# The first projection of the last MLP as seven block products instead of eight

## Chip, core and metric

The kernel runs on one core of one Trainium2 chip. The metric is the device time of one execution in microseconds (us). TensorE (PE) multiplies, VectorE (DVE), ScalarE (ACT) and GpSimd (POOL) do the rest, and SyncE (SP) issues most DMA transfers.

## What is computed

512 tokens of width 1024 pass a retention layer, a latent attention layer, and a block that ends in an MLP. Everything is float32 at the interface. The part that the change touches, cut from the reference:

```
h = rmsnorm(x, norm_mlp_g[l])
x = x + jnp.square(jax.nn.relu(h @ w_up[l])) @ w_down[l]   # h 512x1024, w_up 1024x4096
return rmsnorm(x, final_g)
```

## The kernel before

Every float32 product is made of three faster ones. An operand is split into a rounded part (hi) and the remainder (lo), and PE adds hi·hi, hi·lo and lo·hi in PSUM: `split_dots`, three matmuls of a 128x128 stationary tile. ACT makes hi by a rounding copy (`split_hi`, `copy`), POOL or DVE makes lo = value − hi (`split_lo`, `lo_of`). Weights come in panels of 128x2048 values (1 MB) through two stage tiles: SP loads a panel, ACT writes `whi`, POOL writes `wlo`, PE uses both. There is no scheduler: each engine runs the instructions in the order in which its part of the program is written, and semaphores hold it back.

The stages, in order of time: four heads of the retention layer (panels 0 to 23, six for each head), its output product AO, the latent attention with its output product BO, the local attention, the output product of the block (panels `WO` to `WO+3`), its norm, then the MLP: the first projection (panels `UP` to `UP+15`) and the second projection, DN.

AO, BO and DN are already made as seven block products in place of eight (Strassen's scheme in Winograd's form). Sums of weight blocks are made during earlier stages in DRAM: ACT copies blocks to `tsum` (`copy_blocks`), POOL adds others to them with accumulating DMA transfers (`sum_step`), of which each waits on a count of landed copies, `t_copy`. DVE makes the sums of the activation blocks.

The first projection is plain. 32 output tiles of 128 features are each the sum of 8 tiles along k, times 512 tokens: 24 matmuls 512 columns wide. The first three tiles are made in two halves of 256 tokens, because the tokens arrive a quarter at a time: DVE adds the last product to the residual (`gather(q)`), ACT sums the squares and takes the root (`root_mean_square(q)`), DVE scales (`scale(q)`, written to `h2_tok`), PE turns the quarter (`turn_x`, 8 transposes of 128x128), ACT rounds it to `xhi` and DVE writes `xlo` (`transposed(q)`). PE turns quarters 0 and 1 while it still multiplies for `WO`, begins the projection on them, and turns quarters 2 and 3 after 48 matmuls of it. For each tile ACT applies the relu from PSUM (`hidden`) and DVE squares it into `hid` (`squared`). Stage 3, `whi_a`, `wlo_a` hold a third set of weights where needed.

Of the kernel before, what the change touches and what calls it, by code (L numbers as in the profile page):

```python
# [64 lines left out]
APART = (B0, L0, UP)  # L65

# [4 lines left out]
Seven = namedtuple("Seven", "dq at w sums ready banks")  # L71
AO = Seven(2, 0, END, 0, (8, 8, 8, 8), ((0, 1), (2, 3), (4, 5), (6, 7), (0, 1), (2, 3), (6, 7)))
BO = Seven(2, 14, END + 8, 8, (28, 28, 28, 28), ((2, 3), (4, 5), (6, 7), (0, 1), (2, 3), (4, 5), (6, 7)))
DN = Seven(4, 28, END + 16, 16, (28, 28, 28, 32), ((4, 5), (6, 7), (0, 1), (2, 3), (4, 5), (6, 7), (0, 1)))
# [45 lines left out]
def program(nc, t, out):  # L120
    with ExitStack() as ctx:
# [144 lines left out]
        with ExitStack() as h:  # L266
            hid = sb("hid", [P, KF, SEQ], F32, h)
            gap("gap_dr", 1, h)
            relu = sb("relu", [P, 4, SEQ], F32, h)
            dx = relu[:, :, :].rearrange("p (f a) n -> p f a n", f=2)  # L270
            dr_hi = sb("dr_hi", [P, 2, PK, HALF], F32R, h)
            dr_lo = sb("dr_lo", [P, 2, PK, HALF], F32R, h)
            stage3 = sb("stage3", [P, PAN], F32, h)

# [200 lines left out]

        def seven_stage(st, d):

            i = own_panel(st) % 2
            return ((stage[i], stage[1 - i], stage2) if st is not DN else (stage3, stage[i], stage[1 - i]))[d % 3]

        def seven_parts(st, d):

            if st is DN:
                hi, lo = ((whi_a, wlo_a), parts(END), parts(END + 1))[d % 3]
            else:
                hi, lo = ((whi[0], wlo[0]), (whi[1], wlo[1]), (whi_a, wlo_a))[d % 3]
            return hi[:, 0:PAN], lo[:, 0:PAN]

# [41 lines left out]
        def _(sp):  # L530
# [122 lines left out]
        def _(pool):  # L653
# [27 lines left out]

            def weights_lo(st, d):
# [82 lines left out]
        def _(pe):  # L765
# [95 lines left out]
            def seven(st, d, blocks, dst=None, c0=0, c1=512, start=False):  # L861
# [4 lines left out]
                pe.wait_ge(d_slo, st.at + d + 1)  # L866
# [431 lines left out]
            for s in range(2):  # L1298

                pe.wait_ge(xt_lo, 3 * KX + 4 * (s + 1))  # L1300
                r = slice(256 * s, 256 * s + 256)
                for m in range(3):
                    if s == 0 and m == 2:
                        turn_x(h2_tok, r_h, TT, 2)
                        turn_x(h2_tok, r_h, TT, 3)
                    wh, wl = panel(UP + m // 2, KX)
                    for k in range(KX):
                        if s == 0 and m % 2 == 0:
                            need(UP + m // 2, 0, KX, k)
# [5 lines left out]
            tiles(UP + 1, 0, KX, bank[2:], (xhi, xlo), 1, 2, nothing, u_m)
            with pe.Fori(0, KF // 4 - 1) as i:
                for a in range(2):

                    tiles(UP + 2 + a, 2 * i, KX, bank[2 * a:], (xhi, xlo), 0, 2,
# [1363 lines left out]
```

## Time and profile before

| | |
|---|---|
| median of 3 runs | 1422.03 us (1421.27 to 1422.37) |
| the profiled execution | 1423.6 us, span 1421.8 us |
| busy in the span | PE 1409.0, DVE 798.3, ACT 647.5, POOL 444.1 us |
| mean granted TensorE clock | 0.997 of full speed |
| DMA | 239.14 MB, 168 GB/s over the span |

Times in the trace run from the start of the span; the execution's own time is 1.8 us longer than its span. A row of a timeline gives start, duration, engine, line, tile written and tiles read, and in brackets how long the engine had been idle and what ended that. The duration of a matmul contains its way through the array, so consecutive matmuls overlap and their starts give the pace.

### The profile page before, as it was taken

The numbers are of one execution on the slowest core, as the hardware profiler recorded it, in microseconds if no ns is written. First come the engines' busy times: TensorE is split into PE (matmuls) and PEld (weight loads), VectorE is DVE, ScalarE is ACT, GpSimd is POOL, SyncE is SP. The second block draws the span as 40 slices with busy tenths as digits, with TensorE's granted clock in tenths as the row PEclk, the third lists the DMA queues.
The fourth block names the chain that finished last, engine by engine and source line by source line (L and its number), as shares of the span: only waits on it lengthen the run. The fifth ranks groups of instructions, "written<-read, shape, count | busy, mean of one in ns | idle before, by whom it ended". The sixth has DMA issues, their size and how long they took to land.

```text
span 1421.8 us, 18290 instructions
## 1 busy us (share of the span) xinstructions
PE 1409.0 (99%) x6940; PEld 1192.6 (84%) x6940; DVE 798.3 (56%) x1366; ACT 647.5 (46%) x1043; POOL 444.1 (31%) x211
## 2 busy tenths in 40 slices
PE   9999999999999999999999999999999999999998
PEld 7888888888889888888888888788889888888887
DVE  6444353549952746444545479936864111168896
ACT  4323232246554534433444356648954322346554
POOL 5334353441034433343343230125214544410000
PEclk9999999999999999999999999999999999999999
DMA  7257545417432867956796557354126523345552
GB/s 290 89 207 197 190 131 140 133 42 264 167 119 93 300 169 208 302 154 174 203 298 171 154 209 270 118 203 125 52 66 186 149 89 110 126 148 183 202 184 113
DMA packets 43064, 239.14 MB, mean 168 GB/s; under 512 B 4480, under 2 KB 9216, under 8 KB 16896
## 3 DMA queue, kind: packets, MB, share of 16 engines
q1 hardware_dynamic: 30240, 158.85, 31.4%
q0 software_dynamic: 4608, 33.56, 11.7%
q10 hardware_dynamic: 8160, 46.01, 9.1%
q8 instruction: 33, 0.54, 0.2%
q14 instruction: 23, 0.19, 0.0%
HBM read 231.05 MB, written 74.45 MB: 215 GB/s over the span
## 4 chain that ended last, share of the span: by engine, by line
PE 89%; DVE 7%; ACT 2%; DMA 1%; POOL 1%; issue 1%; SPq 0%; DVEq 0%; ACTq 0%; POOLq 0%
PE bank L524 24%; PE bank L522 24%; PE bank L523 24%; PE bank L1073 6%; PE bank L1035 4%; PE bank L1135 3%; PE bank L1052 1%; DVE wlo L1906 1%; DMA v_spill<-v_tok 1%; DVE wlo_a L1906 1%; PE bank L821 1%; DVE br_lo L1906 1%; PE bank L1215 0%; PE bank L923 0%; POOL wlo L688 0%
## 5 line engine op out<-in xcount | busy, mean ns | idle before, releaser
L660 POOL TENSOR_TENSOR wlo<-stage,whi 128x1024 fp32r<-128x1024 f32 (+1 forms) x146 | 361.8, 2499 | 687.0 <-ACT whi L1347 687.0
L522 PE MATMUL bank<-xhi,whi 128*128 128x512 f32 (+1 forms) x504 | 195.1, 387 | 0.0
L524 PE MATMUL bank<-xhi,wlo 128*128 128x512 f32 (+1 forms) x504 | 194.6, 386 | 0.0
L523 PE MATMUL bank<-xlo,whi 128*128 128x512 f32 (+1 forms) x504 | 194.4, 386 | 0.0
L1347 ACT ACTIVATE whi<-stage 128x1024 fp32r<-128x1024 f32 (+1 forms) x150 | 152.2, 1065 | 80.7 <-PE bank L524 61.8
L524 PEld LDWEIGHTS bank<-xhi,wlo 128*128 128x128 f32 x504 | 94.7, 188 | 19.4
L523 PEld LDWEIGHTS bank<-xlo,whi 128*128 128x128 f32 x504 | 94.7, 188 | 18.9
L522 PEld LDWEIGHTS bank<-xhi,whi 128*128 128x128 f32 x504 | 94.7, 188 | 18.6
L2518 DVE TENSOR_TENSOR hid<-relu 128x512 f32 (+1 forms) x32 | 23.1, 722 | 138.2 <-ACT relu L1841 138.2
L522 PE MATMUL bank<-whi,xhi 128*128 128x512 f32 (+1 forms) x236 | 91.4, 387 | 1.2 <-POOL wlo L660 1.2
L524 PE MATMUL bank<-whi,xlo 128*128 128x512 f32 (+1 forms) x236 | 90.4, 383 | 0.0
L523 PE MATMUL bank<-wlo,xhi 128*128 128x512 f32 (+1 forms) x236 | 90.3, 383 | 0.0
L1906 DVE TENSOR_TENSOR wlo<-stage,whi 128x1024 fp32r<-128x1024 f32 x68 | 81.8, 1218 | 0.0
L1350 ACT ACTIVATE whi<-stage 128x1024 fp32r<-128x1024 f32 (+2 forms) x81 | 78.4, 1013 | 4.2 <-DMA stage<-in_w 4.2
L1841 ACT ACTIVATE relu<-bank 128x512 f32<-128x512 f32 x32 | 19.1, 598 | 117.8 <-PE bank L524 117.8
L522 PEld LDWEIGHTS bank<-whi,xhi 128*128 128x128 f32 x236 | 44.8, 190 | 10.6 <-POOL wlo L660 1.3
L524 PEld LDWEIGHTS bank<-whi,xlo 128*128 128x128 f32 x236 | 44.8, 190 | 8.4
L523 PEld LDWEIGHTS bank<-wlo,xhi 128*128 128x128 f32 x236 | 44.9, 190 | 8.0
L1073 PE MATMUL bank<-xhi,whi 128*128 128x512 f32 x128 | 50.6, 396 | 0.0
L1073 PE MATMUL bank<-xhi,wlo 128*128 128x512 f32 x128 | 50.1, 391 | 0.0
L1073 PE MATMUL bank<-xlo,whi 128*128 128x512 f32 x128 | 49.9, 390 | 0.0
L1906 DVE TENSOR_TENSOR wlo_a<-stage,whi_a 128x1024 fp32r<-128x1024 f32 x40 | 47.8, 1218 | 0.0
(404 smaller groups left out, 3540.5 us busy)
## 6 DMA issues: line engine op xcount, KB each, us to landing
stage<-in_w SPq DMA_DIRECT2D x95, 1024.0 KB, 4.8
tsum<-in_w ACTq DMA_DIRECT2D x32, 1024.0 KB, 13.9
stage<-tsum SPq DMA_DIRECT2D x32, 1024.0 KB, 4.8
tsum<-in_w POOLq DMA_DIRECT2D x16, 1024.0 KB, 10.0
tsum<-tsum POOLq DMA_DIRECT2D x16, 1024.0 KB, 9.9
stage<-in_w SPq DMA_DIRECT2D x8, 1152.0 KB, 6.1
o_spill<-gt SPq DMA_DIRECT2D x16, 256.0 KB, 10.7
bT<-o_spill SPq DMA_DIRECT2D x4, 1024.0 KB, 6.9
```

Of the source, the lines that this page charges most:

```text
L522: pe.matmul(dst, a_hi, b_hi, start=start, stop=False)
L523: pe.matmul(dst, a_hi, b_lo, start=False, stop=False)
L524: return pe.matmul(dst, a_lo, b_hi, start=False, stop=stop)
L660: pool.tensor_tensor(lo[:, r], stage[p % 2][:, r], hi[:, r].bitcast(F32), ALU.subtract).then_inc(w_lo, 1)
L1035: last = pe.matmul(bank[4 + q][:, 0:w], left, right, start=i == 0, stop=i == 4)
L1073: last = pe.matmul(bank[0][:, :], left[:, k, f], right[:, k, :], start=i == 0, stop=i == 23)
L1135: last = pe.matmul(bank[m][:, :], left[:, k, m * P:(m + 1) * P], right[:, k, :], start=i == 0, stop=i == 23)
L1347: act.activation(parts(p)[0][:, r], stage[p % 2][:, r], ACT.Copy).then_inc(w_hi, 1)
L1350: act.activation(dst, src, ACT.Copy, scale=scale).then_inc(signal, 1)
L1841: act.activation(relu[:, m, :], bank[m][:, :], ACT.Relu).then_inc(u_r, 1)
L1906: dve.tensor_tensor(dst, src, hi.bitcast(F32), ALU.subtract).then_inc(signal, 1)
L2518: dve.tensor_tensor(hid[:, bass.ds(4 * i + m, 1), :].rearrange("p a n -> p (a n)"), relu[:, m, :], relu[:, m, :], ALU.mult).then_inc(u_s, 1)
```

## The change

The projection is written as seven block products. Tokens are split in two halves of 256, k in two halves of 512, the 4096 features in two halves of 2048. For each of 16 pairs of feature tiles (one tile in either half) PE makes seven products of 4 tiles along k and 256 tokens, `up_product(i, f)`, each 12 matmuls of 256 columns. The pair's weights come as two rows, n = 2i with products 2, 5, 4, 3 and n = 2i+1 with 0, 1, 6, through three sets of stage, hi and lo (`up_set`).

Of the four weight sums two are made in DRAM (`usum`: `copy_b11`, `copy_b22` on ACT's queue, `up_sum` on POOL, all during the retention heads) and two by DVE in the stage tiles (`up_t2`, `up_t4`). All lo parts of these weights are now DVE's (`up_lo`). The block sums of the activations (r1, s3, s2, s4) are made by DVE from the turned quarters in PSUM and from plain copies that ACT writes (`up_x`, `up_a21`); their hi parts are ACT's (`sum_hi`) and their lo parts DVE's (`sum_lo`). Results are combined from PSUM by one ACT copy (`keep_eighth`) and seven DVE operations of 256 columns (`eighths`); relu and square are ACT's (`hidden`). The last four steps of the sums for DN on POOL, the banks of DN and its three sets move too.

```diff
+UP_ROW = ((2, 5, 4, 3), (0, 1, 6))
+UP_TURN = (4, 2, 3, 5, 0, 1, 6)
+UP_FIRST = (4, 0, 6, 3, 2, 5, 1)
...
+            def up_load(n):
...
+                elif n < 3:
+                    sp.wait_ge(w_lo, 2 * (WO + 2 + n))
+                else:
+                    sp.wait_ge(d_tlo, 2 * (UA + n - 2))
...
-                    sum_step(AO, p - 8 if p < 12 else p - 12, (4, 8), 0)
+                    sum_step(AO, p - 8 if p < 12 else p - 12, (8, 20), 4)
+                elif 12 <= p < 16 or 20 <= p < 24:
+                    up_sum(p // 20, p % 4)
...
+            def up_product(i, f):
+
+                n, c0 = (2 * i + 1, UP_ROW[1].index(f)) if f in UP_ROW[1] else (2 * i, UP_ROW[0].index(f))
+                pe.wait_ge(d_tlo, 2 * (UA + n) + 2)
+                if i == 0:
+                    pe.wait_ge(xt_lo, 3 * KX + {4: 4, 0: 4, 6: 6, 3: 7, 2: 8, 5: 9, 1: 10}[f])
...
+                for kk in range(PK):
+                    c = slice(512 * c0 + kk * P, 512 * c0 + (kk + 1) * P)
+                    last = split_dots(pe, bank[4 * (i % 2) + b][:, half * HALF:(half + 1) * HALF], wh[:, c], wl[:, c],
+                                      x_hi[:, kk, :], x_lo[:, kk, :], kk == 0, kk == PK - 1)
...
+            turn_x(h2_tok, r_h, TT, 2)
+            pe.wait_ge(xt_hi, 3 * KX + 8)
+            for i in range(UPN):
+                if i >= 2:
+                    pe.wait_ge(u_r, i - 1)
+                for k, f in enumerate(UP_TURN if i else UP_FIRST):
+                    if i == 0 and k == 2:
                         turn_x(h2_tok, r_h, TT, 3)
...
# ACT
+            def up_hi(n):
+
+                act.wait_ge(d_ld[(UA + n) % 3], loads(UA + n))
+                act.wait_ge(d_sum, up_sums(n // 2) + n % 2 + 1)
+                if n >= 3:
+                    act.wait_ge(u_m, n - 2)
+                for r in up_halves(n):
+                    copy(up_set(n)[1][:, r], up_set(n)[0][:, r], d_thi)
...
                 if h == 2:
                     act.wait_ge(t_sum, 16)
                     copy_blocks(AO, 1, 3)
+                    copy_b22()
...
                 if h == 0:
                     copy_blocks(AO, 0, 2)
+                    copy_b11()
...
                 if ln is None:
-                    split_hi(next_panel)
                     root_mean_square(0)
                     root_mean_square(1)
                     transposed(0)
+                    up_hi(0)
                     root_mean_square(2)
                     transposed(1)
-                    split_hi(next_panel + 1, free1, done)
+                    act.wait_ge(half_done, HA + 6)
+                    up_hi(1)
                     root_mean_square(3)
-                    transposed(2)
-                    transposed(3)
+                    second_hi(2)
+                    plain(2)
+                    plain(3)
+                    second_hi(3)
+                    sum_hi(3, up_s2, 5)
...
# DVE
+            def eighths(i):
+
+                dve.wait_ge(u_m, 2 * i + 2)
+                dve.wait_ge(u_s, 5 * i + 1)
...
+            for i in range(1, UPN):
+                up_t2(i)
+                up_t4(i)
+                up_lo(2 * i)
+                if i >= 2:
+                    eighths(i - 2)
+                up_lo(2 * i + 1)
+            eighths(UPN - 2)
             remainders(DN, 0)
-            squared(2, KF // 4 - 1)
             remainders(DN, 1)
-            squared(3, KF // 4 - 1)
+            eighths(UPN - 1)
```

DVE, at the norm in front of the projection, before: the residual additions (line 2024), the scaling of a quarter (2066), the lo parts of the turned quarters (1906).

```order
L2066 SCALAR_TENSOR_TENSOR h2_tok<-xres,small,grow 128x1024 [waits dve_step]
L2024 TENSOR_TENSOR xres<-xres,bank4 128x512 [waits y_done]
L2027 TENSOR_TENSOR xres<-xres,bank5 128x512 [waits dve_step,y_done]
L1906 TENSOR_TENSOR xlo<-bank0,xhi 128x4x128 [waits xt_hi]
L1906 TENSOR_TENSOR xlo<-bank1,xhi 128x4x128 [waits xt_hi]
L2064 RECIPROCAL small<-small 128x1 [waits r_sd]
L2066 SCALAR_TENSOR_TENSOR h2_tok<-xres,small,grow 128x1024 [waits dve_step]
L1906 TENSOR_TENSOR xlo<-bank2,xhi 128x4x128 [waits xt_hi]
L1906 TENSOR_TENSOR xlo<-bank3,xhi 128x4x128 [waits xt_hi]
L2024 TENSOR_TENSOR xres<-xres,bank6 128x512 [waits y_done]
L2027 TENSOR_TENSOR xres<-xres,bank7 128x512 [waits dve_step,y_done]
```

DVE at the same place in the changed kernel, from the lo of quarter 1 to the scaling of quarter 3 (now lines 2034, 2173, 2176, 2215; line 2148 is `up_t4`, line 2239 a block sum).

```order
L2034 TENSOR_TENSOR xlo<-bank3,xhi 128x4x128 [waits xt_hi]
L2148 TENSOR_TENSOR stage1<-stage3 128x512 [waits d_sum,w_lo]
L2034 TENSOR_TENSOR wlo1<-stage1,whi1 128x1024 [waits d_thi]
L2034 TENSOR_TENSOR wlo1<-stage1,whi1 128x512 [waits d_thi]
L2173 TENSOR_TENSOR xres<-xres,bank6 128x512 [waits y_done]
L2176 TENSOR_TENSOR xres<-xres,bank7 128x512 [waits dve_step,y_done]
L2239 TENSOR_TENSOR hid<-hid,bank4 128x4x128 [waits xt_t,xt_hi]
L2213 RECIPROCAL small<-small 128x1 [waits r_sd]
L2215 SCALAR_TENSOR_TENSOR h2_tok<-xres,small,grow 128x1024 [waits dve_step]
```

The work on the weights of pair 0 now stands between the residual additions and the scalings on DVE; likewise `up_lo(0)`, two operations of 1024 columns, stands ahead of the addition for quarter 2.

ACT at the end of head 0 in the changed kernel: the copies of weight blocks in DRAM, then the next head.

```order
L1420 ACTIVATE whi1<-stage1 128x1024
L1471 DMA tsum<-in_w 128x2048 x4
L1476 DMA usum<-in_w 128x2048 x4
L1591 DMA decay<-in_decay 128x512 [waits a_dec]
L1420 ACTIVATE whi0<-stage0 128x1024 [waits a_qk,landed0]
```

The second of these DMA rows is new; the four transfers follow the four of before on one queue, and POOL's first `sum_step` counts all eight.

## Rows read from the trace of the kernel before

**Rows 1.** The page: busy time of each engine; the chain that ended last, by engine

```profile
PE 1409.0 (99%) x6940; PEld 1192.6 (84%) x6940; DVE 798.3 (56%) x1366; ACT 647.5 (46%) x1043; POOL 444.1 (31%) x211
PE 89%; DVE 7%; ACT 2%; DMA 1%; POOL 1%; issue 1%; SPq 0%; DVEq 0%; ACTq 0%; POOLq 0%
```

**Rows 2.** Waits of PE, whole span: us in total, times, longest

```profile
PE bank L821 <- DVE h_tok L2066: 2.0, 1, 2.0
```

**Rows 3.** Timeline of PE: a quarter turned; the projection's first matmuls, 256 columns

```profile
1083.36 1.03 PE L821 MATMUL bank<-ident,h_tok 128*128 128x128 f32 x8
...
1087.00 0.28 PE L522 MATMUL bank<-xhi,whi_a 128*128 128x256 f32 x1
```

**Rows 4.** Timeline of ACT: relu of consecutive tiles, 24 matmuls apart

```profile
1103.33 0.60 ACT L1841 ACTIVATE relu<-bank 128x512 f32<-128x512 f32 x1 [2.28 <-PE bank L524]
...
1106.21 0.60 ACT L1841 ACTIVATE relu<-bank 128x512 f32<-128x512 f32 x1 [0.39 <-PE bank L524]
1111.67 0.60 ACT L1841 ACTIVATE relu<-bank 128x512 f32<-128x512 f32 x1 [4.87 <-PE bank L524]
```

**Rows 5.** Timeline of PE: first matmul of DN

```profile
1263.79 0.39 PE L522 MATMUL bank<-whi_a,dr_hi 128*128 128x512 f32 x1
```

**Rows 6.** Busy time in a stretch of the projection: us, then each engine's

```profile
1107.00:1258.00 151.00, 151.00 (x668) 125.04 (x667) 23.60 (x31) 43.60 (x56) 66.58 (x30) 1.00 0.36 118
```

**Rows 7.** Timeline of DVE at the norm: addition, scaling, lo parts, scaling

```profile
1079.92 0.69 DVE L2027 TENSOR_TENSOR xres<-xres,bank 128x512 f32<-128x512 f32 x1 [0.31 <-PE bank L524]
...
1083.04 1.28 DVE L2066 SCALAR_TENSOR_TENSOR h_tok<-xres,small,grow 128x1024 f32<-128x1024 f32 x1
1084.63 1.29 DVE L1906 TENSOR_TENSOR xlo<-bank,xhi 128x512 fp32r<-128x512 f32 x2 [0.30 <-ACT xhi L1350]
...
1089.63 2.34 DVE L2066 SCALAR_TENSOR_TENSOR h_tok<-xres,small,grow 128x1024 f32<-128x1024 f32 x1
```

**Rows 8.** Timeline of ACT at the norm: squares, root, rounding of a quarter, of weights

```profile
1076.01 1.05 ACT L1405 ACTIVATE h_tok<-xres 128x1024 f32<-128x1024 f32 x1
1076.96 0.18 ACT L1405 ACTIVATION_READ_ACCUMULATOR h_tok<-xres 128x1 f32 x1
1077.18 0.29 ACT L1408 ACTIVATE small<-small,eps 128x1 f32<-128x1 f32 x1
1080.36 1.08 ACT L1350 ACTIVATE xhi<-bank 128x512 fp32r<-128x512 f32 x2 [2.88 <-PE bank L821]
...
1084.97 2.01 ACT L1347 ACTIVATE whi<-stage 128x1024 fp32r<-128x1024 f32 x2
```

**Rows 9.** Timeline of DVE near DN: lo parts of weights, 1024 columns each

```profile
1261.28 2.35 DVE L1906 TENSOR_TENSOR wlo<-stage,whi 128x1024 fp32r<-128x1024 f32 x2
```

**Rows 10.** Timeline of PE at an earlier norm; a stretch, granted clock behind POOL

```profile
919.14 1.40 PE L821 MATMUL bank<-ident,h_tok 128*128 128x128 f32 x8 [1.97 <-DVE h_tok L2066]
...
920.00:926.00 6.00, 4.77 (x12) 3.10 (x11) 5.96 (x6) 2.75 (x6) 4.62 (x2) 0.50 0.14 19
```

**Rows 11.** Groups by line and shape: DVE operation on 256 columns in PSUM

```profile
L2481 DVE CUSTOM_DVE_ANT_1 bank<-bank,bias 128x256 f32<-128x256 f32 x32 | 13.1, 443 | 1.5 <-PE bank L1202 1.3
```

**Rows 12.** Copies in DRAM after head 0: last issues; busy and DMA while they run

```profile
85.65 1.18 ACTq L1389 DMA_DIRECT2D tsum<-in_w  x2
86.87 0.61 ACTq L1475 DMA_DIRECT2D decay<-in_decay  x1
...
85.00:102.00 17.00, 17.00 (x79) 14.17 (x78) 8.01 (x11) 4.04 (x5) 8.98 (x4) 1.00 0.94 324
```

**Rows 13.** Timeline of POOL in head 1: lo of panels 8 and 9, DMA between

```profile
97.78 5.21 POOL L660 TENSOR_TENSOR wlo<-stage,whi 128x1024 fp32r<-128x1024 f32 x2 [7.49 <-ACT whi L1347]
102.93 0.95 POOL L668 DMA_DIRECT2D tsum<-in_w  x1
108.67 5.20 POOL L660 TENSOR_TENSOR wlo<-stage,whi 128x1024 fp32r<-128x1024 f32 x2 [4.79 <-ACT whi L1347]
```

**Rows 14.** Timeline of ACT: hi of panel 10, once PE is done with panel 8

```profile
118.40 2.01 ACT L1347 ACTIVATE whi<-stage 128x1024 fp32r<-128x1024 f32 x2 [3.32 <-PE bank L524]
```

More of the change, by code:

```diff
@@ L268, in program @@
             gap("gap_dr", 1, h)
-            relu = sb("relu", [P, 4, SEQ], F32, h)
-            dx = relu[:, :, :].rearrange("p (f a) n -> p f a n", f=2)
+            with ExitStack() as f:
+                eight = sb("eight", [P, 4, HALF], F32, f)
+                s2u_lo = sb("s2u_lo", [P, PK, HALF], F32R, f)
+            dx = sb("dx", [P, 2, 2, 512], F32, h)
             dr_hi = sb("dr_hi", [P, 2, PK, HALF], F32R, h)
@@ L1315, in _ @@
[L1315 to L1319, printed above, removed]
-                          lambda m: pe.wait_ge(u_r, 4 * i + (2 * a + m + 5)), u_m)
+            def up_product(i, f):
[3 more added lines that the diff above has]
+                    pe.wait_ge(xt_lo, 3 * KX + {4: 4, 0: 4, 6: 6, 3: 7, 2: 8, 5: 9, 1: 10}[f])
+                b, half = UP_BANK[f]
+                wh, wl = up_set(n)[1:]
+                x_hi, x_lo = up_operand(f)
+                for kk in range(PK):
+                    c = slice(512 * c0 + kk * P, 512 * c0 + (kk + 1) * P)
+                    last = split_dots(pe, bank[4 * (i % 2) + b][:, half * HALF:(half + 1) * HALF], wh[:, c], wl[:, c],
+                                      x_hi[:, kk, :], x_lo[:, kk, :], kk == 0, kk == PK - 1)
+                return last
@@ L1830, in _ @@
             split_hi(WO + 3, half_done, HA + 5)
-            norms(2 * TT, rms=1, squares_to=h2_tok, round_=3, next_panel=UP, free1=half_done, done=HA + 6)
+            norms(2 * TT, rms=1, squares_to=h2_tok, round_=3)
             act.wait_ge(r_h, 2 * TT)
             act.dma_start(grow[:, :], t["grow"][2]).then_inc(aux["grow"], 16)
-            def hidden(m, i, split=True):
-                act.wait_ge(u_m, 4 * i + (m + 1))
-                act.wait_ge(u_s, 4 * i + (m + 1))
-                act.activation(relu[:, m, :], bank[m][:, :], ACT.Relu).then_inc(u_r, 1)
-                if m % 2 and split:
-                    split_hi(UP + 2 + m // 2, u_m, 4 * i + (m + 1), PAN, 2 * i)
@@ L1845, in _, with keep_eighth @@
-            with act.Fori(0, KF // 4 - 1) as i:
-                for m in range(4):
-                    hidden(m, i)
-            hidden(0, KF // 4 - 1, False)
-            hidden(1, KF // 4 - 1, False)
-            act.wait_ge(u_s, 4 + PK)
-            rounded(DN, 0)
-            hidden(2, KF // 4 - 1, False)
-            act.wait_ge(u_s, 4 + 2 * PK)
-            rounded(DN, 1)
-            hidden(3, KF // 4 - 1, False)
-            act.wait_ge(u_m, KF)
-            for d in range(2, 7 * DN.dq):
+            def keep_eighth(i):
+                act.wait_ge(u_m, 2 * i + 2)
+                if i:
+                    act.wait_ge(u_r, i)
+                copy(kept_eighth, bank[4 * (i % 2) + UP_BANK[0][0]][:, 0:HALF], u_s)
@@ new lines, in hidden @@
+            def hidden(i):
+                act.wait_ge(u_r, i + 1)
+                for h in range(2):
+                    act.activation(hid[:, UPN * h + i, :], eight[:, 2 * h:2 * h + 2, :].rearrange("p a n -> p (a n)"),
+                                   ACT.Relu, scale=1.0 - 2 * h).then_inc(u_s, 1)
+                for h in range(2):
+                    act.wait_ge(u_s, 5 * i + h + 2)
+                    act.activation(hid[:, UPN * h + i, :], hid[:, UPN * h + i, :], ACT.Square).then_inc(u_s, 1)
@@ L1858, in _ @@
+            for i in range(1, UPN):
+                up_hi(2 * i)
+                if i >= 2:
+                    keep_eighth(i - 2)
+                up_hi(2 * i + 1)
+                if i >= 2:
+                    hidden(i - 2)
+            keep_eighth(UPN - 2)
+            hidden(UPN - 2)
+            for d in range(7 * DN.dq):
                 f, g = divmod(d, DN.dq)
                 if f == 0:
-                    act.wait_ge(u_s, 4 + PK * (g + 1))
+                    act.wait_ge(u_s, 5 * (4 * g + 3) + 4)
@@ L2084, in norms @@
                     transposed(1)
+                    up_t4(0)
+                    up_lo(1)
                     gather(3)
+                    s3(2)
                     scale(3)
-                    transposed(2)
-                    transposed(3)
+                    s2(2, 1)
+                    second_lo(2)
+                    r1(2)
+                    s3(3)
+                    s2(3, 4)
+                    second_lo(3)
+                    sum_lo(3, up_s2, 13)
+                    r1(3)
+                    s4(2)
+                    s4(3)
+                    sum_lo(2, up_r1, 14)
+                    sum_lo(5, up_s4, 15)
+                    sum_lo(1, up_s3, 16)
                 elif rms is None:
@@ L2676 @@
     t["o_spill"] = nc.dram_tensor("o_spill", (HB, P, SEQ), F32).ap()
+    t["usum"] = nc.dram_tensor("usum", (2, 4, P, PAN), F32).ap()
     t["tsum"] = nc.dram_tensor("tsum", (32, P, PAN), F32).ap()
```

237 lines of the change are left out of this document (173 added, 64 removed).

## The prediction

> **What bounds the kernel now.** I read the page's busy times first: PE is busy for 1409.0 of 1421.8 us, and the chain that ended last lies on PE for 89% of the span [rows 1]. PE's list of waits then says what is left to gain elsewhere: the longest is 2.0 us, for a scaled quarter at an earlier norm [rows 2]. So the time is the number of matmuls times their pace, and any new wait of PE is added in full. The projection and its turns take from 1087.00 [rows 3] to 1263.79, where DN begins [rows 5]: 176.8 us. In it ACT and DVE are lightly loaded: of 151 us, DVE works 23.6, ACT 43.6, POOL 66.6 [rows 6].
>
> **What PE saves.** The pace is read from the relus of consecutive tiles: a tile of two halves is 24 matmuls of 256 columns and takes 2.88 us, so 0.120 each; a tile of 512 columns takes 5.46, so 0.227 each [rows 4]. Before: 144 matmuls of 256, 696 of 512 and the turns of quarters 2 and 3 (two of some 0.87): 17.3 + 158.0 + 1.75 = 177, against the 176.8 read above. After: 16 pairs × 7 products × 12 = 1344 matmuls of 256, 161.3 us, and the same 1.75: 163.0. Against the stretch as read, PE works **13.8 us less**. That is less than an eighth, since a half-width matmul costs 53% of a full one.
>
> A rule of the Trainium skill (TensorE: Matmul & The Clock Gate, on back-to-back matmuls) has the pace at N ÷ 2.4 GHz + about 2.5 ns, 109 ns at 256 columns and 216 at 512. By it the saving would be some 19 us. The rows show 120 and 227, and the sum goes by them.
>
> **What the start loses.** Before, PE had 5.8 us of products on quarters 0 and 1 as cover while quarters 2 and 3 were scaled. Now it turns quarter 2 first, and has one product, 1.44 us, before it needs the second row of weights, whose lo part DVE writes itself. I follow the order of the rows in the change section, with the prices of [rows 7 to 9]: DVE 0.69 for 512 columns (1.29 for two), 2.35 for two of 1024, 1.28 for a scaling and 0.2 for its reciprocal; ACT 0.54 for a copy of 512 in a series, 1.05 for one of 1024, 1.5 for squares, their read-out and root.
>
> Up to quarter 2: ACT begins on quarter 0 at 1080.4 as before [rows 8]. It now makes four copies (2.1), then the hi of row 0 (1.05 to the first half): 1083.6. DVE waits for it, writes two lo halves (2.35), 1085.9; only then the two additions (1.4), 1087.3; ACT squares and root, 1088.9; DVE scaling, 1090.4. Before, this scaling began at 1083.04 [rows 7]; now PE, done at 1087.0, idles **3.4 us**.
>
> Up to quarter 3: DVE lo of quarter 1 (1.29), `up_t4` (0.69), ACT's hi (1.05), DVE's lo (1.14 + 0.69): 1095.2, when product 0 can begin. Additions 1.4, squares and root 1.5, two ACT copies 1.15, block sum 0.62, reciprocal and scaling 1.5: 1101.4. PE turns quarter 3 then, 14.4 us after 1087.0, and has worked 3.8 of them.
>
> Up to pair 1: turning (0.87 to 1.4), 1102.8; ACT's plain copy 0.6; DVE s3, s2, lo (0.69 each): product 6 begins at 1105.5. Now DVE's queue decides: one lo of a sum (waits for its hi, to 1107.0), r1 and two s4 (1.9), three lo of 1024 (3.4), 1112.3; `up_t2` (0.69), ACT's hi 1.05, two lo 2.35: pair 1 begins at **1116.5**. Without a wait it would begin at 1087.0 + 1.75 + 7 × 1.44 = 1098.8. The start costs **17.7 us**, more than PE saves.
>
> The clock adds little here. At an earlier norm PE idled 1.97 us before eight transposes; the stretch behind, 920 to 926, ran at 0.50 of the clock, which is 1.2 GHz, and the transposes took 1.40 in place of about 1.0 [rows 3, 10]. The new idle times are longer, so I expect 1.2 GHz from about 1090 and back to 2.4 some 5 us after product 6 begins. Of this only the turn of quarter 3 is on the path (0.5, in the sum above): the products of pair 0 end at about 1115, before DVE releases pair 1.
>
> **The loop is covered.** A pair is 10.08 us of PE. DVE: two sums (1.4), lo of 1024 three times (3.4) and of 512 (0.6), seven operations of 256 columns. The nearest of these took 0.443 [rows 11], four of them wait for the one ahead: 2.9. Together 8.3. ACT: 3.5 hi halves, one copy, four of 512: 6. The weights of a row are rounded when PE leaves the row three back, 10.08 us ahead; that takes 4.5. So no wait in 15 pairs, and POOL, which worked 4.8 us a panel, is idle. Loads of 0.5 to 0.8 MB instead of 1 MB are ahead by a pair.
>
> **The handover to DN.** DN's first operand needs tiles that are free once product 5 of pair 15 is done, 4.3 us before DN. ACT needs 1.05 for the operand, DVE follows with 3.4: just in time, 0 (bounds 0 and 0.5). Then `eighths(15)` (3.2) and relu and squares (2.1) stand between step 1 and step 2 of DN on DVE and ACT. From the start of DN: DVE ends step 1 at 3.6, `eighths` at 6.6, ACT's four at 8.6, operand and first weights of step 2 with lo parts at 12.1, against 10.9 when PE wants it. **1.2 us** (0.6 if a 256-column operation takes 0.36, 3.1 if 0.6).
>
> **The head stage.** After head 0 ACT's queue carries four more 1 MB copies, and POOL's first `sum_step`, behind the lo of panel 8, waits for all eight. Before, the four copies, one panel and the decay tile were 5.5 MB in 17 us, at 94% of the DMA engines: 324 GB/s [rows 12]. Four more are 4.2 MB, 12.9 us, and the load of panel 10 shares 3 us of that: landed at about 116.5, where POOL stood free at 102.93 [rows 13]. Issue 0.9, lo halves at 119.9 and 122.2. PE begins panel 9 at about 118.3 [rows 14] and wants the second half 1.4 us later: 1.6 + 0.9, **2.5 us** (bounds 0, if the copies land 3 us sooner; 6, if they run at half rate against the panel load). Head 2 carries eight more halves, but POOL's sum there comes 40 us after the copies start, not 19: 0. The accumulating transfers on POOL cost 0.9 each in idle time of POOL: 0. AO reads its sums at 317, the last new sum is issued before 300: 0.
>
> **Sum.** −13.8 + 17.7 + 1.2 + 2.5 = +7.6 on 1423.6 us: 1431.2 for an execution like the profiled one. That one stood 1.6 over the median of the runs, so the median should be **1429.6 us**. The measurement can tell about 0.2% (2.8 us) from no change.
>
> **Rivals.**
> *The low clock lasts.* If short waits in pair 0 keep PE at 1.2 GHz through pair 1 too, its 84 matmuls cost 0.213 each in place of 0.120: 7.8 more, 1437. For it: several idle times of 1 to 4 us in 30. Against: at 921.5 PE was back within 5 us of steady work. Chance 0.12.
> *The start chain is half as long (faster).* If the waits at the start sum to under 10.1 us, the kernel is faster: that needs DVE's queue from product 6 to pair 1 hidden, and the scalings not held by the weight work. With 8 us and no wait in the head: 1417. Against: the queue order on DVE is fixed. 0.07.
> *Both small costs hidden, the start a little shorter (15 us).* 1423.3 to 1424.5: no change. For it: bounds of 0 above. 0.13.
> *DVE bounds the loop.* From 0.67 us for each 256-column operation on, a pair takes longer than 10.08; at 0.8 it is some 1 us a pair, 1445. Against: 0.443 [rows 11]. 0.04.
> *A narrow matmul costs just half a wide one in the loop,* 0.1135 in place of 0.120: 1344 × 0.0065 = 8.7 less, 1420.9. The rows of the same shape on the same engine stand against it. 0.02. The rule of the Trainium skill (TensorE: Matmul & The Clock Gate, back-to-back matmuls) would go further, to 109 ns and 14.8 less.
> The forecast itself has 0.62.
>
> Range: the forecast's own bounds are −3 at the start, 0 for the head and 0 for DN below, and +3 for the start, +2 for DN, +2 for the head above: 1423 to 1437 also takes in most of the clock rival and of no change. Slower 0.78, no change 0.13, faster 0.09.
>
> **What would show it.** In the changed trace: 256-column matmuls at 0.120 all through the loop and pairs 10.08 us apart; turns of quarters 2 and 3 near 1093 and 1104 (2.5 later by the head's wait), pair 1 near 1119; a clock of 0.50 between; PE waiting for POOL's lo in head 1 with POOL waiting for a copy to `tsum` or `usum`; a short wait at step 2 of DN. Wrong would be: pair 1 beginning before 1115, or waits in the loop.

## The result and the profile after

The changed kernel takes **1440.09 us** (median of 4 runs, 1438.71 to 1440.94) beside 1422.2 us of the kernel before on the same chip: a ratio of 1.0125 with a 95% interval of 1.0107 to 1.0142. It is slower, as forecast, but by 17.9 us instead of 7.6, and the time lies 3 us above the range. The profiled execution took 1440.58 us, its span 1438.8 us.

The page of the kernel after, busy time and the chain that ended last by engine, as in [rows 1]:

```profile
PE 1405.5 (98%) x7444; PEld 1212.5 (84%) x7444; DVE 907.4 (63%) x1552; ACT 699.3 (49%) x1131; POOL 373.5 (26%) x187
PE 82%; DVE 8%; ACT 3%; DMA 2%; ACTq 2%; POOL 1%; issue 1%; SPq 0%; DVEq 0%; POOLq 0%
```

PE is busy for only 3.5 us less, not 13.8: part of its work ran at the lower clock (mean granted clock 0.990, before 0.997). ACTq, the DMA issues that ACT makes, had 0% of the chain before and now has 2%. PE's list of waits (us in total, times, longest), where [rows 2] had 2.0 as its longest:

```profile
PE bank L564 <- POOL wlo L721: 10.2, 5, 5.6
PE bank L891 <- DVE h_tok L2215: 9.4, 3, 4.3
PE bank L564 <- DVE wlo L2034: 3.0, 3, 1.3
PE bank L564 <- DVE xlo L2034: 2.6, 2, 2.4
```

The forecast knows the last three rows (one of the three waits in the second is that of [rows 2], at the earlier norm); of the first it had 2.5 us. Where the time goes is read from an instruction that both kernels have in every head, ACT's rounding of the gate. First before, then after: the last of head 0, the first of the stretch behind head 1's start, the same behind head 2's.

```profile
83.91 0.60 ACT L1496 ACTIVATE gate<-bank 128x512 f32<-128x512 f32 x1 [4.85 <-PE bank L524]
...
138.52 0.60 ACT L1496 ACTIVATE gate<-bank 128x512 f32<-128x512 f32 x1 [4.90 <-PE bank L524]
...
216.32 0.60 ACT L1496 ACTIVATE gate<-bank 128x512 f32<-128x512 f32 x1 [4.90 <-PE bank L524]
```

```profile
84.44 0.60 ACT L1613 ACTIVATE gate<-bank 128x512 f32<-128x512 f32 x1 [4.85 <-PE bank L566]
...
143.90 0.60 ACT L1613 ACTIVATE gate<-bank 128x512 f32<-128x512 f32 x1 [4.89 <-PE bank L566]
...
230.02 0.60 ACT L1613 ACTIVATE gate<-bank 128x512 f32<-128x512 f32 x1 [4.90 <-PE bank L566]
```

The changed kernel is late by 0.53, 5.38 and 13.70 us. So head 1 costs 4.85 us and head 2 costs **8.3 us**, for which the forecast had nothing. At the norm of the MLP the turn that stood at 1083.36 [rows 3] stands at 1094.79: late by 11.4. The 2.3 us between come back on the way, most of them at two places. Both kernels wait 2.0 us at the earlier norm and then run at the low clock, but the kernel after for a shorter time. Its turn and a stretch behind it, to be compared with [rows 10]:

```profile
932.61 1.09 PE L891 MATMUL bank<-ident,h_tok 128*128 128x128 f32 x8 [2.00 <-DVE h_tok L2215]
...
936.00:938.00 2.00, 1.71 (x5) 0.81 (x3) 1.97 (x4) 0.00 (x0) 2.00 (x1) 0.50 0.00 0
```

The granted clock is 0.76 in the 2 us ahead of that stretch and 0.89 in the 2 us behind it, where the kernel before has 0.50 for 6 us; behind this place the lateness is 12.7. Some 50 us later the kernel before waits 1.0 us for DVE (`nz`) and the kernel after does not; the lateness falls to 11.4. Why either differs was not looked for. From the norm of the MLP to the end of the span (17.0 us later than before) the change costs another 5.6.

**Head 2.** Timeline of the issues and engines in the kernel after (ACTq rows are DMA issues), then busy time in a stretch as in [rows 6], then the piece of the chain of waits that carries it (start, duration, what):

```profile
171.09 21.45 ACTq L1481 DMA_DIRECT2D usum<-in_w  x8
...
192.65 2.00 ACT L1420 ACTIVATE whi<-stage 128x1024 fp32r<-128x1024 f32 x2 [23.07 <-issue]
...
193.78 5.14 POOL L721 TENSOR_TENSOR wlo<-stage,whi 128x1024 fp32r<-128x1024 f32 x2 [19.54 <-ACT whi L1420]
...
180.00:200.00 20.00, 14.41 (x56) 11.11 (x55) 8.23 (x9) 4.93 (x6) 6.22 (x4) 0.86 1.02 306
```

```profile
174.22 13.28 ACTq L1481
```

The eight issues of `copy_b22` hold ACT for 21.45 us, the fifth of them for 13.28. Behind them in ACT's order stands the hi of the next panel, and behind that POOL's lo and PE's matmuls. PE waits once, 5.6 us, until 196.19, and the mean granted clock is 0.86 in the 20 us around it: 8.3 in all. The low clock comes behind the wait:

```profile
196.00:198.00 2.00, 1.81 (x4) 1.49 (x5) 2.00 (x2) 1.58 (x2) 2.00 (x2) 0.50 1.07 249
```

**Head 1.** The four issues of `copy_b11`, POOL's first `sum_step`, which answers to the second of [rows 13], the stretch behind PE's two waits (2.5 and 0.5 us), and 2 us of it, at 1.2 GHz:

```profile
87.38 2.61 ACTq L1476 DMA_DIRECT2D usum<-in_w  x4
...
117.89 0.96 POOL L729 DMA_DIRECT2D tsum<-in_w  x1 [14.37 <-DMA usum<-in_w]
...
120.00:135.00 15.00, 13.20 (x51) 10.40 (x52) 2.08 (x3) 3.13 (x5) 10.00 (x6) 0.89 0.98 246
...
124.00:126.00 2.00, 2.00 (x6) 1.52 (x6) 0.00 (x0) 0.00 (x0) 0.05 (x1) 0.50 0.87 205
```

**The start of the projection.** Timeline of PE (the last row is pair 1's first matmul), and the busy time in three stretches:

```profile
1101.65 1.40 PE L891 MATMUL bank<-ident,h_tok 128*128 128x128 f32 x8 [3.07 <-DVE h_tok L2215]
...
1106.48 0.38 PE L564 MATMUL bank<-xhi,whi 128*128 128x256 f32 x1 [0.64 <-DVE wlo L2034]
...
1112.47 1.95 PE L891 MATMUL bank<-ident,h_tok 128*128 128x128 f32 x8 [4.29 <-DVE h_tok L2215]
...
1116.78 0.55 PE L564 MATMUL bank<-xhi,whi 128*128 128x256 f32 x1 [2.36 <-DVE xlo L2034]
...
1127.88 0.39 PE L564 MATMUL bank<-xhi,whi 128*128 128x256 f32 x1 [1.03 <-DVE wlo L2034]
...
1087.00:1110.00 23.00, 17.46 (x91) 14.50 (x90) 14.01 (x19) 12.82 (x25) 0.00 (x0) 0.93 0.17 46
1110.00:1130.00 20.00, 14.14 (x85) 13.57 (x86) 18.16 (x23) 9.09 (x11) 0.00 (x0) 0.74 0.17 55
1130.00:1280.00 150.00, 150.00 (x1249) 149.87 (x1248) 118.97 (x193) 90.75 (x137) 3.32 (x4) 1.00 0.59 165
```

The waits on turns and pair 1 are those of the forecast, and the loop behind them has no idle time of PE in 150 us, with DVE busy for 119 of them. DN's first matmul and its first wait:

```profile
1279.17 0.40 PE L564 MATMUL bank<-whi,dr_hi 128*128 128x512 f32 x1
...
1291.53 0.47 PE L564 MATMUL bank<-whi,s_hi 128*128 128x512 f32 x1 [1.28 <-DVE wlo L2034]
```

### The profile page after: what moved, and what is told of

It is laid out like the page before. It is cut to its first block, busy times and chain, and to the rows that moved or that the text cites. A ratio compares the mean times of both kernels' runs of the same rounds, so it can differ in the third digit from the quotient of the medians.

```text
span 1438.8 us, 19392 instructions
## 1 busy us (share of the span) xinstructions
PE 1405.5 (98%) x7444; PEld 1212.5 (84%) x7444; DVE 907.4 (63%) x1552; ACT 699.3 (49%) x1131; POOL 373.5 (26%) x187
## 3 DMA queue, kind: packets, MB, share of 16 engines
q10 hardware_dynamic: 10912, 54.40, 10.8%
## 4 chain that ended last, share of the span: by engine, by line
PE 82%; DVE 8%; ACT 3%; DMA 2%; ACTq 2%; POOL 1%; issue 1%; SPq 0%; DVEq 0%; POOLq 0%
PE bank L564 22%; PE bank L565 21%; PE bank L566 21%; PE bank L1143 6%; PE bank L1205 4%; PE bank L1105 4%; DMA usum<-in_w 2%; DVE wlo L2034 2%; ACTq L1481 1%; PE bank L1122 1%; POOL wlo L721 1%; DVE wlo_a L2034 1%; DVE br_lo L2034 1%; PE bank L891 1%; PE bank L1285 0%
## 5 line engine op out<-in xcount | busy, mean ns | idle before, releaser
L721 POOL TENSOR_TENSOR wlo<-stage,whi 128x1024 fp32r<-128x1024 f32 (+2 forms) x116 | 290.1, 2531 | 566.1 <-ACT whi L1420 566.1
L1420 ACT ACTIVATE whi<-stage 128x1024 fp32r<-128x1024 f32 (+2 forms) x120 | 122.2, 1068 | 94.9 <-PE bank L566 48.1
L564 PE MATMUL bank<-xhi,whi 128*128 128x512 f32 (+1 forms) x428 | 149.8, 350 | 4.0 <-DVE xlo L2034 2.4
L566 PE MATMUL bank<-xhi,wlo 128*128 128x512 f32 (+1 forms) x428 | 149.0, 348 | 0.0
L565 PE MATMUL bank<-xlo,whi 128*128 128x512 f32 (+1 forms) x428 | 148.8, 348 | 0.0
L1423 ACT ACTIVATE whi<-stage 128x1024 fp32r<-128x1024 f32 (+2 forms) x125 | 117.9, 989 | 47.5 <-PE bank L566 32.7
L2034 DVE TENSOR_TENSOR wlo<-stage,whi 128x1024 fp32r<-128x1024 f32 x112 | 127.7, 1167 | 17.6 <-ACT whi L1423 17.6
L564 PEld LDWEIGHTS bank<-xhi,whi 128*128 128x128 f32 x428 | 81.6, 191 | 14.7 <-issue 2.7
L2034 DVE TENSOR_TENSOR wlo_a<-stage,whi_a 128x1024 fp32r<-128x1024 f32 (+1 forms) x60 | 68.8, 1175 | 12.1 <-ACT whi_a L1423 12.1
L1423 ACT ACTIVATE whi_a<-stage 128x1024 fp32r<-128x1024 f32 (+1 forms) x56 | 53.8, 1010 | 16.5 <-PE bank L566 14.3
L2034 DVE TENSOR_TENSOR pt_lo<-bank,pt_hi 128x384 fp32r<-128x384 f32 (+1 forms) x48 | 26.6, 596 | 35.6 <-ACT pt_hi L1423 35.6
```

Of the source, the lines that this page charges most:

```text
L564: pe.matmul(dst, a_hi, b_hi, start=start, stop=False)
L565: pe.matmul(dst, a_hi, b_lo, start=False, stop=False)
L566: return pe.matmul(dst, a_lo, b_hi, start=False, stop=stop)
L721: pool.tensor_tensor(lo[:, r], stage[p % 2][:, r], hi[:, r].bitcast(F32), ALU.subtract).then_inc(w_lo, 1)
L1420: act.activation(parts(p)[0][:, r], stage[p % 2][:, r], ACT.Copy).then_inc(w_hi, 1)
L1423: act.activation(dst, src, ACT.Copy, scale=scale).then_inc(signal, 1)
```

## The experiments

Theory: the 10.5 us over the forecast are head 2, ACT held at its own DMA issues, plus a stretch at 1.2 GHz behind each of the two waits in the heads. First rival: head 2 is POOL's count, as in head 1. Second rival: DRAM traffic, whoever issues it. Third: the start of the projection cost more than the forecast's 17.7.

**1. A count of their own for the new copies.** `sum_step` no longer waits for the copies to `usum`.

```diff
-                pool.wait_ge(t_copy, 16 * ((8, 20)[k] + 1))
+                pool.wait_ge(u_copy, 16 * (4, 12)[k])
...
-                    sum_step(AO, p - 8 if p < 12 else p - 12, (8, 20), 4)
+                    sum_step(AO, p - 8 if p < 12 else p - 12, (4, 8), 4)
```

> The copies for the projection's sums get a semaphore count of their own, so that GpSimd's first sum step in head 1 waits for the four old copies only; the bytes stay. Theory (the wait costs it): the wait of 14.4 us on GpSimd goes, and with it TensorE's 2.5 and 0.5 us on panel 9 and the stretch at 1.2 GHz behind it, 4.9 us of shift in all: 1435.2 us. Head 2 keeps its 8.3. Rival (the bytes cost it): with the accumulating transfers now running beside the copies the panel loads come late and TensorE still loses 3 us or more in head 1: 1438 or more.

Measured: 1436.3 us (1435.53 to 1436.88), ratio 1.0096 [1.0079, 1.0113], beside 1422.1. In this kernel POOL's issue in head 1 and ACT's in head 2 read:

```profile
103.29 0.95 POOL L730 DMA_DIRECT2D tsum<-in_w  x1
```

```profile
165.48 21.43 ACTq L1482 DMA_DIRECT2D usum<-in_w  x8
...
120.00:135.00 15.00, 15.00 (x75) 12.81 (x74) 6.10 (x9) 7.96 (x12) 10.11 (x6) 1.00 0.99 286
180.00:200.00 20.00, 14.99 (x56) 11.52 (x55) 10.27 (x8) 5.53 (x7) 10.67 (x5) 0.83 1.04 322
```

Head 1's cost is gone and its clock is 1.00, with the DMA engines as full as ever. Head 2 is untouched: the first rival falls.

**2 and 3. The second block with longer rows.** The block b22 is laid out once more as an input, so that it can be copied in rows of 8 KB, as four transfers of 1 MB (first), or as eight of 512 KB with runs of 4 KB (second), instead of eight with runs of 2 KB. A run is a piece that lies without a gap. The bytes are the same. The edit of the first:

```diff
-                for j in range(8):
-                    act.dma_start(t["usum"][1, j // 2, :, 1024 * (j % 2):1024 * (j % 2) + 1024].rearrange(
-                        "p (a n) -> p a n", a=2),
-                        t["w"][UP + 8 + j, :, 0:PAN].rearrange("p (a n) -> p a n", a=2)[:, :, 0:512]).then_inc(t_copy, 16)
+                for g in range(4):
+                    act.dma_start(t["usum"][1, g, :, :], t["b22"][g, :, 0:PAN]).then_inc(t_copy, 16)
```

> The second block is copied from rows of 8 KB in four transfers of 1 MB, as the first one is, in place of eight of 512 KB in runs of 2 KB; the same bytes at the same place. Theory (ScalarE stands at its DMA issues, since many short pieces fill its queue): the eight issues took 21.5 us with one of 13.3, now four take under 4 us, the hi of panel 14 is in time, and the 8.3 us that head 2 lost are back: 1431.8 us. Rival (12 copies crowd the DMA engines, and panels land late): the bytes are the same, so head 2 loses what it lost: 1440 us.

> Eight transfers of 512 KB as in the change, but in runs of 4 KB on both sides, half as many pieces. If the number of pieces fills the queue, the issues take clearly less than 21.5 us and at least half of the 8.3 us comes back: 1432 to 1436. If the number of transfers does, the issues take about as long as in the change: 1440.

Measured: four transfers 1432.2 us (1429.22 to 1433.32), ratio 1.0066 [1.0049, 1.0083]; eight 1433.4 us (1432.76 to 1435.02), ratio 1.0079 [1.0062, 1.0096]. The rows of the version with four, then of that with eight:

```profile
170.14 2.57 ACTq L1481 DMA_DIRECT2D usum<-in_b  x4
...
179.23 2.01 ACT L1420 ACTIVATE whi<-stage 128x1024 fp32r<-128x1024 f32 x2 [10.24 <-PE bank L566]
...
180.00:200.00 20.00, 20.00 (x90) 16.57 (x89) 15.61 (x15) 5.78 (x8) 11.24 (x5) 1.00 1.02 327
```

```profile
169.25 16.29 ACTq L1482 DMA_DIRECT2D usum<-in_b  x8
...
185.64 2.01 ACT L1420 ACTIVATE whi<-stage 128x1024 fp32r<-128x1024 f32 x2 [16.89 <-issue]
```

With four transfers ACT is free after 2.57 us, its hi waits for PE as it should, and PE has no wait in head 2 while the DMA engines are full all the same (share 1.02). So it is not the traffic: the second rival falls. With eight the issues still take 16.29 us, but hi comes 7 us sooner than in the changed kernel, and PE waits 0.9 us in head 2.

**4 and 5. The copies alone, in the kernel before.** The kernel before with the new copies and sums in the heads, which nobody reads; once as the change has them, once mended (a count of their own, and four transfers of 1 MB in rows of 8 KB in place of the eight halves). Of the edit as the change has them:

```diff
+            def copy_b11():
+
+                for g in range(4):
+                    act.dma_start(t["usum"][0, g, :, :], t["w"][UP + 4 + g, :, 0:PAN]).then_inc(t_copy, 16)
...
+                    copy_b22()
...
+                elif 12 <= p < 16 or 20 <= p < 24:
+                    up_sum(p // 20, p % 4)
```

> The kernel before, with the change's copies and sums in DRAM added at their places and with their counts; nothing reads them. Theory (the heads' loss is the copies' alone): heads 1 and 2 lose 4.9 + 8.3 as in the change: 1435.4 us. Rival (part of the loss comes from the projection's end of the kernel): under 1431.

> The kernel before with the copies and sums in DRAM that nothing reads, but in the mended form of e5. If moving 12 MB more beside the heads costs nothing once no engine waits for it, 1422.2 us (within 0.2%); if the traffic itself costs, 1425 or more.

Measured: as in the change 1435.6 us (1434.95 to 1437.74) beside 1422.1, ratio 1.0097 [1.0080, 1.0114]; mended 1423.24 us (1422.05 to 1424.22) beside 1422.5, ratio 1.0002 [0.9992, 1.0011]. The unmended kernel loses its time without one new product: the issues are there again, `168.40 21.99 ACTq`, and POOL's waits. So the heads' cost has nothing to do with the projection, and 16.8 MB of new traffic (the page of the profile counts 255.92 MB for 239.14; the expectation said 12) by itself costs nothing that can be measured.

**6. Both mends in the changed kernel** (edits 1 and 2 together).

> The change with both mends of the retention heads: a count of their own for the new copies, and the second block copied in four transfers with rows of 8 KB. If the two losses are separate and all that the heads cost, 4.9 + 8.3 us come back: 1426.9 us, which is the forecast sum without its 2.5 for head 1 (1427.1). The residue over the kernel before, 4.7 us, is then start chain (17.7) and handover (1.3) less TensorE's saving (13.8). Rival (the losses hide behind one another): over 1429.

Measured: 1428.2 us (1426.66 to 1429.08) beside 1422.5, ratio 1.0038 [1.0023, 1.0052]. What is left is the projection's own cost. The forecast less its 2.5 for head 1 is 1427.1 for exactly this kernel. The third rival falls.

**7. A shorter start.** Both mends, and in the start: `up_hi(0)` goes ahead of the first squares on ACT, `up_t4(0)` ahead of the norm, quarter 3's scaling ahead of the block sum on DVE, and the lo halves of rows 0 and 1 go to POOL.

```diff
+            for n in range(2):
+                hi, lo = up_set(n)[1:]
+                for b, r in enumerate(up_halves(n)):
+                    pool.wait_ge(d_thi, 2 * (UA + n) + b + 1)
+                    pool.tensor_tensor(lo[:, r], up_set(n)[0][:, r], hi[:, r].bitcast(F32), ALU.subtract).then_inc(d_tlo, 1)
...
-                    up_lo(0)
...
-                    up_t4(0)
-                    up_lo(1)
                     gather(3)
-                    s3(2)
                     scale(3)
+                    s3(2)
```

> As e5, and at the norm: the hi of weight row 0 ahead of the squares on ScalarE, the second weight sum ahead of the norm, the lo parts of rows 0 and 1 on idle GpSimd, and the scaling of quarter 3 ahead of the first block sum on VectorE. Theory (the start is lost in VectorE's and ScalarE's order, where weight work stands between the additions and the scalings): quarters 2 and 3 are turned some 3 and 9 us sooner, pair 1 begins 9 us sooner: 1418 us, faster than the kernel before. Rival (the start is bound by the block sums and their lo parts alone, whatever stands ahead): the queue behind product 6 is as long as it was and pair 1 comes under 4 us sooner: over 1423.

Measured: **1419.66 us** (1418.65 to 1424.0) beside 1422.5, ratio 0.9981 [0.9967, 0.9995]. PE's waits at the start are now 1.3 (POOL's lo), 3.2 (quarter 3's lo) and 1.9 us (pair 1).

**8 and 9. A third row on POOL, and back.** From the last kernel, pair 1's two weight sums `up_t2(1)`, `up_t4(1)` go between the addition and the scaling of quarter 3, `up_hi(2)` goes ahead on ACT, and row 2's lo goes to POOL. Then the same with row 2's lo on DVE.

```diff
-            for n in range(2):
+            for n in range(3):
...
+                    up_t2(1)
+                    up_t4(1)
                     scale(3)
```

```diff
-            for n in range(3):
+            for n in range(2):
...
                     sum_lo(1, up_s3, 16)
+                    up_lo(2)
```

> As e6, and both sums of row 2 and 3 while VectorE waits for quarter 3's root, the hi of row 2 behind the first operand sum on ScalarE and its lo on GpSimd. Theory: pair 1 no longer waits for two sums, a hi and two lo on VectorE, only for the end of pair 0: 1.5 to 2.5 us off e6, 1416. Rival: products of pair 0 wait for the lo parts of the block sums to the same moment, and row 2 was not the last thing: within 0.5 of e6.

> The order with row 1's reductions ahead of the scaling and rows 0 and 1's lo halves on POOL, but with row 2's lo back on VectorE, behind the eighth block's lo sum. Theory (VectorE's operations with all operands in SBUF stretch while POOL runs a tensor_tensor): the two subtractions of row 3's normalisation, 5.04 us beside POOL before, take 1.28 us again, and the kernel gains some 3 to 4 us: about 1421. Rival (the order itself is what cost, POOL or not): the same as with POOL on row 2, 1424.8.

What the second text calls reductions are the weight sums `up_t2(1)` and `up_t4(1)`; its two subtractions of 5.04 us are block sums of the activations (line 2247).

Measured: three rows on POOL 1424.8 us (1421.99 to 1428.65), ratio 1.0011 [1.0001, 1.0022], 8.8 us over what I expected; row 2 on DVE 1419.41 us (1417.15 to 1419.97) beside 1422.55, ratio 0.9976 [0.9967, 0.9986]. The timeline of DVE and of POOL with three rows on POOL:

```profile
1088.14 1.94 DVE L2146 TENSOR_TENSOR stage<-stage 128x512 f32<-128x512 f32 x1
...
1099.45 0.68 DVE L2247 TENSOR_TENSOR hid<-bank,hid 128x512 f32<-128x512 f32 x1
1100.06 5.04 DVE L2247 TENSOR_TENSOR hid<-hid 128x512 f32<-128x512 f32 x2
```

```profile
1087.13 4.07 POOL L834 TENSOR_TENSOR wlo<-stage,whi 128x1024 fp32r<-128x1024 f32 x2 [12.79 <-ACT whi L1429]
1099.30 5.24 POOL L834 TENSOR_TENSOR wlo<-stage,whi 128x1024 fp32r<-128x1024 f32 x2 [8.10 <-ACT whi L1429]
```

and of DVE with row 2 back on DVE:

```profile
1097.15 1.28 DVE L2247 TENSOR_TENSOR hid<-hid 128x512 f32<-128x512 f32 x2
```

Two block sums whose operands all lie in SBUF take 5.04 us beside POOL's subtraction and 1.28 without it. The block sum just ahead of them, begun beside POOL too but with one operand in PSUM (`bank`), keeps its 0.68. A rule of the Trainium skill (SBUF — State Buffer, on who interferes with whom) says this: a VectorE instruction with two SBUF inputs contends with a GpSimd instruction that reads SBUF, and one with at most one, outside VectorE's 2-port modes, does not. The trace agrees, by 5.04 against 1.28 and by the 0.68 that stayed. The order alone was innocent, and POOL's help on row 2 cost more than it gave.

**10 and 11. The sums earlier, and only one row on POOL.** In the first of these, `up_t2(1)` and `up_t4(1)` move behind quarter 1's scaling, where POOL is idle; in the second, row 1's lo goes back to DVE as well, ahead of quarter 3's addition.

```diff
                     scale(1)
+                    up_t2(1)
+                    up_t4(1)
                     gather(2)
...
-                    up_t2(1)
-                    up_t4(1)
                     scale(3)
```

> As the kernel before in this list, but the two reductions of row 1 moved from the place where POOL computes row 1's lo to behind row 1's scaling, where POOL is idle. Theory (shared stretch): they take their short time, pair 1's first matmul comes about 2 us sooner than in the kernel with two lo halves on POOL and the old order, and the time is about 1418. Rival (the last block's data, not VectorE, sets pair 1): no gain on 1419.7.

> As the second of this list, but row 1's lo is on VectorE too, ahead of row 3's gather, and only row 0's on POOL. The stretch by POOL is gone from row 3's scaling (1.28 us instead of about 1.9), while VectorE has one more subtraction of about 0.7 to 1.3 us on the path to the last row: within 1 us of the second of this list, about 1418. If POOL's work costs VectorE as much as it saves, this one is the faster; if not, the slower by up to 1 us.

Measured: sums early **1417.65 us** (1416.31 to 1419.64), ratio 0.9965 [0.9952, 0.9977]; row 1 on DVE 1418.49 us (1417.55 to 1419.84), ratio 0.9973 [0.9964, 0.9983]. DVE's first weight sum and its scaling with the sums early, then the scaling with row 1 on DVE:

```profile
1079.80 0.68 DVE L2146 TENSOR_TENSOR stage<-stage 128x512 f32<-128x512 f32 x1
...
1090.86 1.87 DVE L2223 SCALAR_TENSOR_TENSOR h_tok<-xres,small,grow 128x1024 f32<-128x1024 f32 x1
```

```profile
1090.54 1.28 DVE L2223 SCALAR_TENSOR_TENSOR h_tok<-xres,small,grow 128x1024 f32<-128x1024 f32 x1
```

The weight sum takes 0.68 where it took 1.94 beside POOL. From quarter 2's turn to pair 1's first matmul it is 20.7 us in experiment 7 and 18.8 here: the expected 2 us. Whether POOL should have row 1 can't be told: 0.8 us apart, with overlapping intervals.

**12 and 13. Transfers or pieces?** In 2 and 3 both were changed together. Here b22 goes as eight transfers of 64 rows of 8 KB (512 pieces in all), and as four transfers cut into runs of 4 KB (1024 pieces); one execution each.

```diff
-                for g in range(4):
-                    act.dma_start(t["usum"][1, g, :, :], t["b22"][g, :, 0:PAN]).then_inc(t_copy, 16)
+                for j in range(8):
+                    q = slice(64 * (j % 2), 64 * (j % 2) + 64)
+                    act.dma_start(t["usum"][1, j // 2, q, :], t["b22"][j // 2, q, 0:PAN]).then_inc(t_copy, 16)
```

> The changed kernel, with the second weight block copied after head 2 as eight transfers of 512 KB as before, but each of 64 rows of 8 KB: as many transfers as in the change and as in the version with 4 KB runs, and as few pieces (512) as in the version with four transfers of 1 MB. If the number of pieces holds ACT up: some 3 to 5 us of issue and no wait of PE in head 2. If the number of transfers does: 16 us or more of issue, as with eight transfers of 4 KB runs.

> The changed kernel, with that block copied as four transfers of 1 MB whose pieces are 4 KB long: as few transfers as in the version with 8 KB rows, and as many pieces (1024) as in the version with eight transfers of 4 KB runs. If the number of pieces holds ACT up: about 16 us of issue, and the hi of the next panel near 185.6. If the number of transfers does: some 2.6 us, and the hi near 179.2.

The issues, in the first and in the second:

```profile
168.89 5.54 ACTq L1482 DMA_DIRECT2D usum<-in_b  x8
```

```profile
168.09 2.83 ACTq L1481 DMA_DIRECT2D usum<-in_b  x4
```

Both are cheap (0.7 us a transfer), and in both PE has no wait in head 2 (1431.54 and 1432.99 us). So neither count alone holds ACT up: 8 transfers are cheap with 512 pieces, 1024 pieces are cheap in 4 transfers, and 8 with 1024 are not. The packets that the pages of the profile count (10912 on ACT's queue in the changed kernel, 9312, 9888, 9376 and 9824 in experiments 2, 3, 12 and 13) fit one account. Four transfers fewer at equal pieces are 64 packets fewer, 16 a transfer; and from the version with four transfers of 8 KB rows to that with 4 KB runs there are 512 more, one for each piece. On ACT's queue stand the decay tile (128 + 16), four copies to `tsum` (4 × 144), then b22. All of the second kernel here: 144 + 576 + 4 × 272 = 1808, issued freely. The changed kernel: 1808 after four of its eight, and the fifth takes 13.28 us. Eight of 4 KB runs: 1728 after seven (the seventh took 1.99), and the eighth (1872) takes 10.30:

```profile
175.23 10.30 ACTq L1482
```

Eight of 8 KB rows: 1360, free. An estimate from these four: some 1,800 packets can be issued to the queue, counted from when it last stood empty, and an issue beyond that waits until older ones have gone. It is not the number still unmoved: 381 packets of the queue had been moved when the 13.28 us began, and 476 when the 10.30 did, so 1,427 and 1,252 were left, while in experiment 13 some 1,470 were left behind the last issue, and it was free. Both long issues ended when some 650 had been moved (665 and 647). No run here varies the number by itself, so the limit, and what counts against it, is argued and not shown.

## Why the prediction was wrong, and where it was right

- **The failed step is the sentence on head 2**: "Head 2 carries eight more halves, but POOL's sum there comes 40 us after the copies start, not 19: 0." It costs 8.3 us. The sum asked only who waits for the copies to land. It did not ask what stands behind the issuing instructions on ACT. One issue took 13.28 us, ACT's next hi came 13 us later than with four transfers, and POOL and PE behind it. Experiment 2 takes this away with the same bytes, and 4 shows it without the change.
- **Head 1: the wait right, the clock left out.** Forecast: copies landed at about 116.5 and 2.5 us of waiting. Measured: POOL went on at 117.9 (0.5 of that was there ahead of head 1), PE waited 3.0. But the stretch behind ran at 0.89, and the head cost 1.9 us more than its waits. The prediction had priced this behaviour at the norm by [rows 10] and not here. Together 4.85 for 2.5.
- **PE's saving right.** Between pair 1 and DN are 15 pairs, 1279.17 − 1127.88 = 151.3 us, 10.09 each, 0.120 a matmul as in [rows 4]. The Trainium skill's rule of 109 ns (TensorE: Matmul & The Clock Gate, on back-to-back matmuls) is not what these matmuls do, at 120. The rival of half a wide one falls too.
- **The start right.** From the end of `WO` (1087.0 before, 11.4 later now, so 1098.4) to pair 1: 29.5 us forecast, 29.5 measured. PE's idle time ahead of quarter 2's turn was forecast at 3.4 and is 3.07; quarter 3's turn was forecast 14.4 us behind the end of `WO` and begins after 14.1. The low clock lay on the path only where it was expected, at the last turn and product 6, and did not outlast pair 0: that rival falls. DVE does not bound the loop; it has 119 of 150 us, and its operations of 256 columns take 0.41 to 0.42, for 0.443.
- **The handover right**: 1.28 us at step 2 of DN, forecast 1.2.
- **Left out of the sum, small:** 0.5 us ahead of head 1, and 2.3 us that come back before the norm of the MLP, mostly at the earlier norm and at the wait for `nz`. The cause of neither was looked for.

With both heads mended (experiment 6) the forecast's other terms give 1427.1 and the chip 1428.2. The two missing terms of the heads are 8.3 and 2.4. That their sum is so near the 10.5 us by which the forecast missed is partly luck. Between the two profiled spans lie 17.0 us, 9.4 more than the forecast's 7.6: 10.7 for the heads, 0.5 ahead of them and 0.5 from the norm on (5.6 for 5.1), less the 2.3 that come back. The other 1.1 lies between single executions and medians: the forecast took 1.6 off for the kernel before, and the profiled execution of the changed one stands 0.5 above its median.

So the scheme is not slow by nature. Its saving of 13.8 us is real, but it came with 17.7 us at the start and 13 in the heads. With the heads mended and the start reordered it beats the kernel before by 4.9 us. Of the other 8.9 us of the saving, 7 lie, as an estimate, between quarter 2's turn and pair 1: 18.8 us (experiment 10), where two turns of 0.87 and seven products of 1.44 would be 11.8.

## What to carry over

A DMA issue is an instruction of its engine: when transfers are added to a queue, read what stands behind them there, count the pieces they are cut in, and prefer few transfers with long rows. Give transfers that different consumers need separate counts, so that adding some delays nobody else. Before work is handed to POOL, see what DVE does in the same microseconds: operations with both inputs in SBUF pay for it.

## What was not expected of the hardware

- One issue of a DRAM copy held ACT for 13.28 us; eight such copies of 512 KB took 21.45 us with 2 KB runs, 16.29 with 4 KB runs, 5.54 with 8 KB rows, and four of 1 MB 2.57 (8 KB) and 2.83 (4 KB).
- A block sum on DVE of two SBUF tiles, 128x512, took 2.5 us beside a subtraction on POOL for 0.64 alone, and a scaling of 128x1024 1.87 for 1.28. That was in sight: [rows 7] has one scaling at 1.28 and one at 2.34, and the prediction took 1.28 for all.
- Waits of PE of 2.5 and 0.5 us in the middle of dense work were followed by a granted clock of 0.50 between 124 and 126 us, and one of 5.6 us by 0.50 from 196 to 200: here the waits, 3.0 and 5.6 us, cost 4.85 and 8.3, about one and a half times their length.
